# Rows of v gathered as 32 picks of four tokens, and summed in four column tiles

## The reference, cut to what matters

```python
q = (xb @ w_pq).reshape(128, 8, 2, 128)
s = einsum('thpd,hpnd->thpn', q, sub_keys)      # scores against 128 keys, twice
top, pos = top_k of the 16 x 16 sums of the two top-16 lists
expert = take_along_axis(cand_idx, pos)         # 16 experts of 16384, per token and head
g = softmax(top)
u, v = u_tab[expert], v_tab[expert]             # rows of 1024 numbers
a = gelu(einsum('td,thkd->thk', xb, u)) * g
out = einsum('thk,thkd->td', a, v)
```

## Time and profile before

| what | us |
|---|---|
| median of 3 runs (lowest, highest) | 5331.91 (5331.56, 5337.48) |
| the profiled execution, device time | 5335.85 |
| its span, first to last instruction | 5334.1 |
| `peer` of layer 0, first u gather to last sums read | 1172.7 to 3214.8 |
| `peer` of layer 1, the same | 4005.8 to 5323.0 |

### The profile page before, as it was taken

The page is one execution under the profiler, slowest core; times in us unless marked ns, Lnnn a source line. Parts: engine busy times, 40 slices in busy tenths (PEclk is TensorE's granted clock), DMA queues, the critical chain, the costliest instruction groups (busy, mean ns, idle before and its releaser), DMA issues.

```text
span 5334.1 us, 50012 instructions
## 1 busy us (share of the span) xinstructions
PE 4580.5 (86%) x14880; PEld 2248.8 (42%) x14880; DVE 2976.1 (56%) x7190; ACT 1065.3 (20%) x2651; POOL 2427.7 (46%) x2576
## 2 busy tenths in 40 slices
PE   4999899978888888888888778899986888888887
PEld 2466655533333333333333333555443333333333
DVE  1554411167676776767766634552137677676764
ACT  0123300012222222222222111231002222222221
POOL 0000000017777777777776540000006777777775
PEclk7999799989999999999999988999998999999999
DMA  7000011339999999999999991000249999999998
GB/s 292 0 20 28 0 42 52 115 115 413 419 416 418 419 408 420 408 415 419 418 419 421 420 392 43 16 31 31 76 160 366 419 413 416 419 411 419 415 419 350
DMA packets 391232, 1506.39 MB, mean 282 GB/s; under 512 B 44408, under 2 KB 45048, under 8 KB 386936
## 3 DMA queue, kind: packets, MB, share of 16 engines
q0 software_dynamic: 368640, 1342.34, 62.0%
q1 hardware_dynamic: 22392, 161.72, 8.0%
HBM read 1501.69 MB, written 2.20 MB: 282 GB/s over the span
## 4 chain that ended last, share of the span: by engine, by line
PE 37%; issue 20%; DMA 20%; POOL 16%; DVE 7%; ACT 1%; SPq 0%; POOLq 0%; DVEq 0%; ACTq 0%
PE ps L480 34%; DMA arena<-in_u_tab,idx 17%; POOL arena L449 8%; POOL arena L459 8%; DVE arena L1310 3%; DMA arena<-in_v_tab,idx 2%; PE ps L587 2%; DMA arena<-in_w_mod 1%; DMA arena<-in_w_qkv 0%; ACT arena L785 0%; DVE arena L1132 0%; DVE mx L1118 0%; DMA mods<-arena 0%; PE ps L512 0%; DVE arena L1243 0%
## 5 line engine op out<-in xcount | busy, mean ns | idle before, releaser
L480 PE MATMUL ps<-arena 128*128 128x512 f32 (+7 forms) x12032 | 4373.1, 520 | 613.8 <-DMA arena<-in_v_tab,idx 416.2
L480 PEld LDWEIGHTS ps<-arena 128*128 128x128 f32 (+1 forms) x12032 | 2059.4, 196 | 2843.1 <-issue 1635.2
L449 POOL DMA_INDIRECT arena<-in_u_tab,idx x1280 | 1212.1, 947 | 2437.2 <-DVE idx L1387 1985.2
L1310 DVE CUSTOM_DVE_ANT_0 arena<-arena,ps 128x1024 f32<-128x1024 f32 x1280 | 1562.6, 1221 | 997.7 <-DMA arena<-in_u_tab,idx 996.3
L459 POOL DMA_INDIRECT arena<-in_v_tab,idx x1280 | 1212.2, 947 | 445.4 <-issue 363.0
L785 ACT COPY arena<-ps 128x256 f32<-128x256 f32 (+3 forms) x518 | 219.4, 429 | 1611.8 <-PE ps L480 881.6
L921 ACT ACTIVATE arena<-ident,coef 128x128 f32<-128x128 f32 x1280 | 382.5, 387 | 375.9 <-DVE coef L1317 375.9
L1236 DVE TENSOR_TENSOR arena<-arena,ps 128x768 f32<-128x768 f32 (+1 forms) x32 | 26.3, 822 | 370.3 <-PE ps L480 370.3
L941 ACT ACTIVATE gl<-dots 128x16 f32<-128x16 f32 x80 | 17.3, 216 | 1003.6 <-DVE dots L1310 1003.6
L1132 DVE COPY arena<-ps 128x384 f32<-128x384 f32 (+1 forms) x128 | 79.9, 624 | 216.3 <-PE ps L587 211.6
L853 ACT ACTIVATE arena<-ps,nm 128x768 f32<-128x768 f32 (+2 forms) x160 | 123.6, 772 | 289.7 <-DVE nm L1122 162.3
(11 more groups left out here) (111 smaller groups left out, 1627.0 us busy)
## 6 DMA issues: line engine op xcount, KB each, us to landing
arena<-in_w_mod SPq DMA_DIRECT2D x24, 2048.0 KB, 11.0
arena<-in_w_gb SPq DMA_DIRECT2D x48, 768.0 KB, 4.2
arena<-in_u_tab,idx POOLq DMA_INDIRECT x1280, 8.2
arena<-in_v_tab,idx POOLq DMA_INDIRECT x1280, 8.2
arena<-in_w_qkv SPq DMA_DIRECT2D x2, 6144.0 KB, 22.2
arena<-in_w_conv SPq DMA_DIRECT2D x24, 512.0 KB, 3.6
arena<-mods SPq DMA_DIRECT2D x21, 512.0 KB, 6.7
arena<-in_w_out SPq DMA_DIRECT2D x2, 4096.0 KB, 13.4
```

Of the source, the lines that this page charges most:

```text
L449: nc.gpsimd.indirect_dma_start(ur[:, row % UR, :], None, u_rows, bass.IndirectOffsetOnAxis(ap=idx[:, at:at + 1], axis=0)).then_inc(u_in[ro ...
L480: return nc.tensor.matmul(o, lhsT, rhs, start=first, stop=last, skip_group_check=True)
L1310: v.tensor_tensor_reduce(u, u, h_cur, 1.0, 0.0, ALU.mult, ALU.add, dots[:, i % 2, k:k + 1]).then_inc(s["dots_done"], 1)
```

## The change

Two heads form a unit of 32 picks. The v gathers run over units: each still brings 128 rows of 4 KB, but these are the 32 picks of four tokens instead of one pick of 128 tokens. For that the indices are turned on PE (`turn_picks`, four matmuls with every fourth column of the identity) and copied back as integers by DVE (`turned_picks`). The coefficients are turned the same way (`turn_coefficients`) and spread by ACT into a zeroed strip, four small copies for a unit (`spread_coefficients`), where 16 diagonals per head were. `sums` takes four gathers at a time: for each half of the columns, four matmuls with 32 columns of weights, each into its own 32 partitions; `v_used` comes in the second half. The v side runs two heads behind u (`LATE`), so the loops have one round more; the end of a tile on DVE is one head later. Two memsets of the strips come at the start of each layer's `peer`.

```diff
@@ peer's gathers
-            def gather_v(i, k):
-                row = TOPK * i + k
+            def gather_v(w, k):
+                row = UNIT * w + k
+                if k == 0:
+                    pool.wait_ge(s["it_done"], w + 1)
                 if row >= VR:
                     pool.wait_ge(s["v_used"], row + 1 - VR)
                 pool.sem_inc(s["pool_turn"], 1)
-                at = i % PH * TOPK + k
+                at = 8 * (k % 4) + k // 4
                 nc.gpsimd.indirect_dma_start(
-                    vr[:, row % VR, :], None, v_rows, bass.IndirectOffsetOnAxis(ap=idx[:, at:at + 1], axis=0)
+                    vr[:, row % VR, :], None, v_rows, bass.IndirectOffsetOnAxis(ap=idxT[:, w % 4, at:at + 1], axis=0)
                 ).then_inc(v_in[row % VR], 16)
...
-                for i in range(heads + 1):
+                for i in range(heads + LATE):
                     for k in range(TOPK):
                         if i < heads:
                             gather_u(i0 + i, k)
-                        if i > 0:
-                            gather_v(i0 + i - 1, k)
+                        if i >= LATE:
+                            gather_v((i0 + i - LATE) // 2, i % 2 * TOPK + k)
@@ TensorE
+            fourth = ident[:].rearrange("p (g q) -> p q g", q=4)
+
+            def turn_picks(w, scored):
...
+                for q in range(4):
+                    m = mm(bank(7, 2 * P, 2 * P + UNIT)[32 * q:32 * q + 32], idxv[:, w % 2, :], fourth[:, q, :])
+                m.then_inc(s["it_mm"], 1)
+
+            def turn_coefficients(w, scored):
+                pe.wait_ge(s["coef_done"], 2 * w + 2)
...
+                for q in range(4):
+                    m = mm(bank(7, 3 * P, 3 * P + UNIT)[32 * q:32 * q + 32], coef[:, w % 2, :], fourth[:, q, :])
+                m.then_inc(s["ct_mm"], 1)
...
             def sums(i, lo, hi):
                 n, h = divmod(i, PH)
-                for k in range(lo, hi):
-                    row = TOPK * i + k
+                w = i // 2
+                if lo == 0 and h == 0:
+                    need(pe, "f_read", n)
+                if lo == 0 and h % 2 == 0:
+                    pe.wait_ge(s["ct_done"], w + 1)
+                for k in range(i % 2 * TOPK + lo, i % 2 * TOPK + hi, 4):
+                    row = UNIT * w + k
                     opens = h == 0 and k == 0
-                    if opens:
-                        need(pe, "f_read", n)
-                    pe.wait_ge(v_in[row % VR], 16 * (row // VR + 1))
-                    pe.wait_ge(s["diag_done"], row + 1)
-                    mm(bank(0), dg[:, k, :], vr[:, row % VR, 0:BW], opens, True)
-                    mm(bank(1), dg[:, k, :], vr[:, row % VR, BW:D], opens, True).then_inc(s["v_used"], 1)
+                    for half in range(2):
+                        for c in range(4):
+                            at = (row + c) % VR
+                            if half == 0:
+                                pe.wait_ge(v_in[at], 16 * ((row + c) // VR + 1))
+                            m = mm(bank(half)[32 * c:32 * c + 32], strip[w % 2][:, c, 8 * k:8 * k + 32],
+                                   vr[:, at, half * BW:(half + 1) * BW], opens, True)
+                            if half == 1:
+                                m.then_inc(s["v_used"], 1)
@@ ScalarE
-            def diagonals(i):
-                act.wait_ge(s["coef_done"], i + 1)
-                for k in range(TOPK):
-                    if i > 0 and k in (0, TOPK // 2):
-                        act.wait_ge(s["v_used"], TOPK * (i - 1) + k + TOPK // 2)
-                    nc.scalar.activation(dg[:, k, :], ident[:], ACT.Copy, scale=coef[:, k:k + 1]
-                                         ).then_inc(s["diag_done"], 1)
+            def spread_coefficients(w):
+                act.wait_ge(s["ct_mm"], w + 1)
+                if w >= 2:
+                    act.wait_ge(s["v_used"], UNIT * (w - 1))
+                for q in range(4):
+                    rows = slice(32 * q, 32 * q + 32)
+                    m = nc.scalar.copy(strip[w % 2][rows, :, q:q + 36 * 7 + 1:36],
+                                       bank(7, 3 * P, 3 * P + UNIT)[rows].rearrange("p (c m) -> p c m", c=4))
+                m.then_inc(s["ct_done"], 1)
@@ VectorE
+            def turned_picks(w):
+                dve.wait_ge(s["it_mm"], w + 1)
+                if w >= 4:
+                    dve.wait_ge(s["v_used"], UNIT * (w - 3))
+                v.tensor_scalar(idxT[:, w % 4, :], bank(7, 2 * P, 2 * P + UNIT), 0.25, None, ALU.add
+                                ).then_inc(s["it_done"], 1)
...
+                    v.tensor_scalar(idxv[:, j // 2 % 2, j % 2 * TOPK:j % 2 * TOPK + TOPK], idxf[:], float(l * EXPERTS), None, ALU.add)
...
+                for b in range(2):
+                    ch.inc(v.memset(strip[b], 0.0))
+                ch.wait()
...
+                        if i % 2 == 1 and k == 3:
+                            turned_picks((i0 + i) // 2)
...
-                        if h == 1 and t > 0:
+                        if h == 2 and t > 0:
                             if k == 3:
                                 ends_read(l, t - 1)
...
-                        if h == 2 and t > 0 and 3 <= k <= 5:
+                        if h == 3 and t > 0 and 3 <= k <= 5:
                             apply_norm(t - 1, k - 3)
-                        if h == 3 and t + 1 < live[l] and 4 <= k <= 5:
-                            next_h(n0 + t + 1, l, t + 1, k - 4)
+                        if h == 3 and t + 1 < live[l] and 8 <= k <= 9:
+                            next_h(n0 + t + 1, l, t + 1, k - 8)
```

More of the change, by code:

```diff
@@ L46 @@
 LEAD = 3
+UNIT = 2 * TOPK
+LATE = 2
 F32 = mybir.dt.float32
@@ L187, in hybrid_dit_peer @@
         hT = region(152, KD, P)
-        dg = region(156, TOPK, P)
+        strip = [region(156 + 4 * b, 4, 2 * P) for b in range(2)]
         q_sb = region(164, 2, P)
@@ L211, in hybrid_dit_peer @@
         gl = sb("gl", [P, TOPK])
-        coef = sb("coef", [P, TOPK])
+        coef = sb("coef", [P, 2, UNIT])
+        idxv = sb("idxv", [P, 2, UNIT])
+        idxT = sb("idxT", [P, 4, UNIT], U32)
         ps = stack.enter_context(nc.psum_tensor("ps", [P, 8 * BW], F32))
@@ L236, in hybrid_dit_peer @@
             "wpq_in keys_in mod2_in end2_in hn_done ht_mm hT_done q_mm q_copied qT_mm qT_copied sc_mm sc_copied "
[L237 removed]
+            "top_done exp_done idx_done gate_done dots_done gelu_done coef_done it_mm it_done ct_mm ct_done v_used pool_turn f_read x_new x_out").split()}
         u_in = [sem(f"u_in{k}") for k in range(UR)]
@@ L723, in key_scores @@
                 m.then_inc(s["sc_mm"], 1)
+            fourth = ident[:].rearrange("p (g q) -> p q g", q=4)
+            def turn_picks(w, scored):
+                need(pe, "idx_done", 2 * w + 2)
+                need(pe, "sc_copied", scored)
+                if w > 0:
+                    pe.wait_ge(s["ct_done"], w)
+                for q in range(4):
+                    m = mm(bank(7, 2 * P, 2 * P + UNIT)[32 * q:32 * q + 32], idxv[:, w % 2, :], fourth[:, q, :])
+                m.then_inc(s["it_mm"], 1)
@@ L746, in peer @@
                     key_scores(i0 + j, j)
-                for i in range(heads + 1):
+                for i in range(heads + LATE):
                     t, h = divmod(i, PH)
                     j = i + LEAD
+                    scored = i0 + min(j, heads)
                     if j < heads:
                         query(i0 + j, j % PH, n0 + j // PH)
-                    if i > 0:
-                        sums(i0 + i - 1, 0, 4)
+                    if i >= LATE:
+                        if i % 2 == 0:
+                            turn_coefficients((i0 + i - LATE) // 2, scored)
+                        sums(i0 + i - LATE, 0, 4)
                     if j < heads:
                         turn_query(i0 + j)
-                    if i > 0:
-                        sums(i0 + i - 1, 4, 8)
+                    if i >= LATE:
+                        sums(i0 + i - LATE, 4, 8)
                     if j < heads:
+                        if i > 0:
+                            pe.wait_ge(s["it_done"], (i0 + i + 1) // 2)
+                        if i >= LATE:
+                            pe.wait_ge(s["ct_done"], (i0 + i) // 2)
                         key_scores(i0 + j, j % PH)
-                    if i > 0:
-                        sums(i0 + i - 1, 8, 12)
+                    if i >= LATE:
+                        sums(i0 + i - LATE, 8, 12)
+                    if i < heads and i % 2 == 0:
+                        turn_picks((i0 + i) // 2, i0 + min(j + 1, heads))
                     if h == PH - 1 - LEAD and t + 1 < live[l]:
                         turn_h(n0 + t + 1)
-                    if i > 0:
-                        sums(i0 + i - 1, 12, TOPK)
+                    if i >= LATE:
+                        sums(i0 + i - LATE, 12, TOPK)
                     m = i - (heads - MODS // 2)
@@ L952, in peer @@
                 exp_top(i0 + 1)
```

(17 more changed lines are left out.)

3 lines of the change are left out of this document (2 added, 1 removed).

## The result

| us | before | changed |
|---|---|---|
| median of 6 runs, same chip | 5334.89 (5331.56 to 5344.98) | 5356.45 (5351.70 to 5358.33) |
| ratio, 95% interval | 1 | 1.0037 [1.0024, 1.0050] |
| span of the profiled execution | 5334.1 | 5354.9 |

What follows compares the result with a forecast made beforehand. The prediction took the DMA's gather rate, equal to POOL's own pace, as the bound, with PE, DVE and ACT waiting for data. Steady part and boundaries 0, layer 1 -1.4, layer 0 -6.7, memsets +3.8: -4.3, so 5328 us, range 5304 to 5352.

Steps and rivals of the forecast that it cites:

- The pace of the middle: Steady pair stream in `peer`: POOL's pitch stays 1.24 to 1.25 us at 419 GB/s; less PE and ACT work changes 0.
- Packing: `sums` matmuls: four strips run at once, 0.108 us a record instead of 0.433, 6.9 us a head instead of 27.7.
- The groups of sixteen in 1.7 to 2 us: Sign of packing in the PE trace: sixteen records of a group should take 1.7 to 2 us.
- A drain at a change of tiling mode: Some ten tiling-mode switches a head on PE: each would add a drain by the skill's rule; costed at no change.
- The start: Each layer's start: second u-only head 26.4 us, first v some 55 us after first u, memsets and index write +1.9.
- The body: First to last u gather of each layer: -13.5 us, a 26.4 us u-only head replacing a 39.9 us pair-stream head.
- The end of layer 1: Last u gather to sums read in layer 1: 52.5 us instead of 40.4, +12.1; layer net -1.4.
- its paragraph on the ring: Eight v buffers released in fours, steady part: 10.2 us from issue to release under five pitches of 12.5, no stall.
- The end of layer 0: From 3160 to the sums read in layer 0: 61.6 us instead of 54.8, +6.8, with 5 idle; layer net -6.7.
- as much as before: Upper bound for layer 0's tail: DMA idle time stays at 18.2 us instead of falling to 5, +13 us.
- PE was holding POOL: Faster rival, v gathers waiting for PE: a faster PE ends over half of up to 45 us, 5303; chance 0.21.
- The four-row release starves the v ring: Slower rival: serial strips, groups over 5 us, v-only gathers 1.73 us, +15 a layer, 5359; 0.21 with slow-clock variant (5348).

Runs made afterwards that it cites:

- e15: The changed kernel unedited, as control on a chip as fast as the first: ratio 1.0032 to the kernel before.
- e2: Changed kernel with the two strip memsets moved behind the first hidden state, on a slow chip: ratio 1.0106 to the kernel before.
- e13: Changed kernel with twelve buffers instead of eight for each layer's last 32 v rows, on a fast chip: ratio 1.0016 to the kernel before.
- e14: Changed kernel with twelve end buffers, release in pairs, memsets behind the first hidden state and `w_qkv` last, fast chip: 5320.79 us, ratio 0.9979 to the kernel before.
- e10: Changed kernel with the `w_qkv` load held back until all v rows of layer 0 are used, slow chip: ratio 1.0108 to the kernel before.
- e12: Kernel before with only the `w_qkv` load held back until all v rows of layer 0 are used, slow chip: ratio 0.9992 to the kernel before.
- e16: Kernel before with only v two heads behind u (`coef` doubled, no packing), repeated on another slow chip: ratio 1.0022 to the kernel before.
- e18: Kernel before with only `w_qkv` held back until layer 0's v rows are all used, repeated on another slow chip: ratio 0.9991 to the kernel before.
- e4: Kernel before with only v two heads behind u (`coef` doubled, no packing), slow chip: ratio 1.0028 to the kernel before.
- e6: The kernel before, unedited, traced on a slow chip: tails 60.7 and 37.0 us; such chips run it in 5762 to 5792 us.
- e7: Changed kernel with v gathers reading untransposed indices, one pick of 128 tokens each (sums of wrong rows), slow chip: ratio 1.0109 to the kernel before.
- e1: Changed kernel with a group's two loops swapped so each row's buffer is released alone, slow chip: ratio 1.0100 to the kernel before.
- e9: Changed kernel with a group's matmuls cut into two pairs, buffers released in twos, slow chip: ratio 1.0092 to the kernel before.

## Why the prediction was wrong

- **The pace of the middle: right.** POOL's pitch, the GB/s and the tiles are as before on the first chip and in e15. Taking a fifth of PE's busy time (262 of 1198 us) and almost half of ACT's out of the middle gained nothing, as neither set the pace.
- **Packing: right in kind.** With all rows there 20 records take 2.83 us (at 3164.51), 0.14 us each, where a record took 0.433 and 0.108 was predicted; with the last rows still landing `x12` take 2.3 to 2.9. The groups of sixteen in 1.7 to 2 us did not show, and PE's 935 busy us in the window are over the 500 to 850 given as a sign: a group's first rows come one by one, two records of 0.5 us for each. POOL's waits for PE in the middle are 15.9 us, 16.6 before. A drain at a change of tiling mode, which the Trainium skill names ("TensorEngine Tiling (Array Packing)", Key Properties), had been weighed and set aside; no row here shows it on the path either.
- **The start: right within 2 us.** The second u-only head took 26.1 us (26.4 predicted) and the first v followed 54.7 and 54.85 us behind the first u (55). A memset took 0.91 us, not 0.87; the stretches before the first u gather grew by 2.75 and 3.1 us, not 1.9. e2 shows 1.1 and 2.8 of it as the memsets'.
- **The body: 4.0 and 2.3 us short.** First tiles are 15.1 and 13.7 us shorter, as predicted or better; the other tiles of a layer sum to 5.6 and 2.6 us more. Tiles of one kernel differ by up to 8 us among themselves, and I can't say what of this is the change.
- **The end of layer 1: this step failed.** "3 x 1.25 + 4.2 (shortest landing) + 2 = 9.95 us for 8 x 1.25 = 10: no more than 1 us lost." The form of the sum is right; the row put into it was not. Landing with v alone is 5.5 to 6.5 us, the round 11.5 to 12.1. And the sum left out the change-over, where five pitches are 6.2 us and no longer the 12.5 of its paragraph on the ring, against a landing of 8.59. From the last u to the last v gather, at 5335.40, POOL took 50.98 us, where the prediction had 39.9 + 1: 10.1 more. Of these the stands make 9 (10.0 us in all, 3.8 of them at the change-over), and 1.1 are a 33rd v gather, the last u's partner, which the sum had forgotten. From there to the read are 8.44 us and not 9.6 + 2: 3.2 less, as the last row lands in 6.5. 12.1 + 10.1 - 3.2 = 19.0, as measured. e13 takes the ring's rounds away and e14 the change-over too.
- **The end of layer 0: this step failed**, with "idle 5 (2 for the last group, 1 ring, 2 for handovers)". The idle time was 15.0 us: the ring in fours again, the change-over (POOL's wait of 6.2 us) and the modulation with the turn of the coefficients (2.9). It came out near its bound, "as much as before" (18.2). How the 15.0 divide among these no run shows. `w_qkv` is no part of the difference on the slower chips (e10, e12).
- **"PE was holding POOL"**: fell. Over the span v gathers waited 97.1 us for PE, 78 times, where it was 60.4, 49 times. The eight waits at tile boundaries did not vanish, but came one head later and a little shorter, 22 us in all where they were 29; the tiles show nothing of it. The one of the earlier trace rows is now:

```profile
2224.38 1.27 POOL L465 DMA_INDIRECT arena<-in_v_tab,idxT  x1 [3.55 <-PE ps L486]
```

- **"The four-row release starves the v ring"**: the right place and a fair size (+15 a layer, measured +10 in layer 1), by the wrong mechanism. I let it begin at "a group of over 5 us"; a group takes 2.3 to 2.9 and it starves all the same, since what decides is three pitches plus landing plus release against eight pitches. A chance hung on PE's speed hung on the wrong quantity.

**Open:** on the slow chips the tiles are 2% longer with the change, and the cause is not found. The lag makes at most 1 to 3 of the 8 us: its tiles are 374.3 (e16) where the kernel before, but for `w_qkv` last, has 373.0 on the same chip (e18), and e4's 373.0 come from a chip that is 0.5% slower than e6's. Order of rows (e7) and clock (e1 and e2) are out. So is, for all that one pair shows, the size of a release: row by row 380.0, in fours 380.3 (e1, e2). In pairs it was 375.9 (e9) against 379.3 (e10). On the fast chips 8.3 of the 25.1 us lie outside the tails, and only the memsets' part of them is shown. The lag alone was not run on a fast chip, nor e14 on a slow one.

## What to carry to other kernels

Where the DMA sets the pace, taking work off the matmul engine gains nothing, and whatever makes the pipeline one stage deeper is paid for at each end at the DMA's rate: here 16 gathers more in each tail, against one head less in the stream, about even only if the tail runs at full rate. A ring that is released in groups runs at full rate only if (group - 1) pitches + landing + time to the first release is under ring x pitch; put in the landing time that such a stretch will have, not the shortest of the trace, look at the change-over by itself (the group that was issued at the old pace and lands in the old time, against the new pitch), and give the ring the buffers that another stream no longer needs. A large load issued within a few us of the last small transfers delays them by nearly its whole length, as the queues share by packets and not by bytes; it belongs behind the last of them if something later can hide it.

## What the runs showed of the hardware

- **Chips differ by 8%.** The same kernel takes 5332 to 5335 us on two chips and 5762 to 5792 on four others; there the middle of the kernel before moves 365 GB/s (e6) and not 417. The change is +0.3 to +0.4% on the former, +1.3% on the one of the latter where it ran.
- **A lower clock without a cost.** The granted clock in the middle fell from 0.99 to 0.84 as PE got gaps, a mix of its two levels (1.2 and 2.4 GHz), and the tiles kept their length; at 0.93 (e14) they are no shorter than at 0.84 (e15).
- **Two DMA queues share by packets.** While the 6 MB load ran, from 3177 to 3183 us, it moved 50 packets of 49 KB and the gathers 48 of 4 KB: 2.46 MB against 0.20.
- **v gathers alone land in 6.3 us** (5.5 to 6.5), with eight buffers; with twelve, in e13, it is 6.6, at most 8.1.
